# Final norm and stores of all rows moved between the last two experts, with expert 14's rows redone by indirect DMA

## The reference, cut to what matters

```python
def expert_choice_ffn(h, w_router, w_gate, w_up, w_down):
    b, n, d = h.shape
    cap = CAPACITY_FACTOR * n // N_EXPERTS          # 64 latent rows, 16 context rows for each expert
    aff = jax.nn.softmax(jnp.einsum('bnd,de->bne', h, w_router).astype(jnp.float32), axis=-1)
    gates, idx = lax.top_k(jnp.swapaxes(aff, 1, 2), cap)
    xe = jax.vmap(lambda hb, ib: hb[ib])(h, idx)
    a = jnp.einsum('becd,edf->becf', xe, w_gate)
    u = jnp.einsum('becd,edf->becf', xe, w_up)
    ye = jnp.einsum('becf,efd->becd', jax.nn.silu(a) * u, w_down) * gates[..., None].astype(h.dtype)
    return jax.vmap(lambda yb, ib: jnp.zeros((n, d), yb.dtype).at[ib.reshape(-1)].add(yb.reshape(-1, d)))(ye, idx)

# in trunk_layer:          x = x + gate2 * expert_choice_ffn(h, *moe_w)
# in reference, at the end: y_prompt = rms_norm(xp, g_final);  y_sample = rms_norm(xs, g_final)
```

## Time and profile before

| what | value |
| --- | --- |
| median of 3 runs | 1146.9 us (1146.23 to 1149.08) |
| the profiled execution's own time | 1145.81 us |
| its span | 1144.0 us |
| PE busy | 1097.6 us, 96% of the span |
| DVE, ACT, POOL busy | 46%, 32%, 12% |
| mean DMA rate | 258 GB/s over the span, about 405 GB/s while the experts run |
| last matmul of the experts starts | 1123.3 us after the span's start |
| last DMA issue on POOL starts | 1135.10 us |

### The profile page before, as it was taken

How to read it: one execution, slowest core, us unless ns; L and a number is a source line. 1 busy time by engine, 2 the same in 40 slices (tenths; PEclk the granted TensorE clock), 3 DMA queues, 4 the chain that set the end, 5 groups by cost and what they waited for, 6 DMA issues and landing times.

```text
span 1144.0 us, 28118 instructions
## 1 busy us (share of the span) xinstructions
PE 1097.6 (96%) x12524; PEld 828.2 (72%) x12524; DVE 528.1 (46%) x961; ACT 363.2 (32%) x846; POOL 132.4 (12%) x173
## 2 busy tenths in 40 slices
PE   6999999999999999999998999999999999999993
PEld 4679875666677777777877877777777777777761
DVE  4574538879958142334976033332233223333235
ACT  4333327778753223022163221222222222211103
POOL 2332300000000000002012111111110111110021
PEclk9999999999999999999999999999999999999997
DMA  9932242111031545359987999999999999999993
GB/s 359 299 107 68 77 84 63 35 31 41 1 109 38 184 147 147 106 190 300 355 303 320 402 398 406 407 405 409 414 406 405 408 404 408 405 408 405 410 321 143
DMA packets 86747, 295.32 MB, mean 258 GB/s; under 512 B 27249, under 2 KB 28530, under 8 KB 62050
## 3 DMA queue, kind: packets, MB, share of 16 engines
q1 hardware_dynamic: 79104, 269.77, 61.5%
q0 software_dynamic: 6528, 20.10, 6.1%
q10 hardware_dynamic: 994, 3.65, 0.9%
HBM read 273.25 MB, written 15.00 MB: 252 GB/s over the span
## 4 chain that ended last, share of the span: by engine, by line
PE 85%; DMA 7%; issue 2%; ACT 2%; DVE 2%; SPq 1%; POOLq 0%; POOL 0%; ACTq 0%; DVEq 0%
PE ps L1207 39%; PE ps L772 10%; PE ps L774 9%; PE ps L773 9%; PE ps L994 4%; PE ps L1013 3%; PE ps L1032 2%; PE ps L1036 2%; DMA x_dram<-y_row,rows_t 2%; DMA x_dram<-xn_p 1%; DMA raw_first<-in_w_in_dram 1%; DMA x_f<-x_dram 1%; PE ps L794 1%; DMA raw<-in_w_in_dram 1%; PE ps L978 1%
## 5 line engine op out<-in xcount | busy, mean ns | idle before, releaser
L2124 DVE SCALAR_TENSOR_TENSOR y_row<-ps,gates,gate_q 32x256 f32<-32x256 f32 (+1 forms) x184 | 88.3, 480 | 238.5 <-PE ps L1207 236.0
L1564 ACT ACTIVATE h_t<-ps 128x256 f32<-128x256 f32 x48 | 15.0, 384 | 374.7 <-PE ps L1207 374.7
L772 PE MATMUL ps<-w_hi,ht 128*128 128x512 f32 (+1 forms) x320 | 124.2, 388 | 0.6 <-DVE q_n L1728 0.6
L774 PE MATMUL ps<-w_hi,ht 128*128 128x512 f32 (+1 forms) x320 | 121.8, 381 | 0.0
L773 PE MATMUL ps<-raw_lo,ht 128*128 128x512 f32 (+1 forms) x320 | 121.7, 380 | 0.0
L1207 PE MATMUL ps<-late,xe 128*32 128x256 f32 x1824 | 103.6, 379 | 0.0
L537 DVE TENSOR_TENSOR raw_lo<-raw,w_hi 128x1024 fp32r<-128x1024 f32 x48 | 58.2, 1234 | 78.9 <-ACT w_hi L532 78.2
L1207 PEld LDWEIGHTS ps<-late,xe 128*32 128x32 f32 x1824 | 77.0, 110 | 23.3
L1207 PE MATMUL ps<-raw,xe 128*32 128x256 f32 x1392 | 88.1, 379 | 0.9 <-issue 0.8
L532 ACT ACTIVATE w_hi<-raw 128x1024 fp32r<-128x1024 f32 x48 | 48.7, 1053 | 123.6 <-DMA raw<-in_w_in_dram 68.1
L2354 POOL DMA_INDIRECT xg<-x_dram,rows x48 | 46.1, 961 | 320.7 <-PE ps L1207 293.2
(11 more groups left out here) (315 smaller groups left out, 1831.0 us busy)
## 6 DMA issues: line engine op xcount, KB each, us to landing
late<-in_w_exp_down_dram SPq DMA_DIRECT2D x25, 1024.0 KB, 20.4
late<-in_w_exp_up_dram SPq DMA_DIRECT2D x21, 1024.0 KB, 28.8
late<-in_w_exp_gate_dram SPq DMA_DIRECT2D x17, 1024.0 KB, 24.7
raw<-in_w_in_dram SPq DMA_DIRECT2D x16, 1024.0 KB, 5.5
raw<-in_w_exp_gate_dram SPq DMA_DIRECT2D x16, 1024.0 KB
raw_gate<-in_w_exp_up_dram SPq DMA_DIRECT2D x14, 1024.0 KB
raw<-in_w_exp_up_dram SPq DMA_DIRECT2D x13, 1024.0 KB
raw_gate<-in_w_exp_down_dram SPq DMA_DIRECT2D x13, 1024.0 KB
```

The lines of the kernel that those rows point to most:

```text
L772: pe.matmul(b, stat_hi(k, tt), hi[:, kk, :], start=first, stop=False)
L774: mm = pe.matmul(b, stat_lo(k, tt), hi[:, kk, :], start=False, stop=last)
L2124: return dve.scalar_tensor_tensor(y_row[n % 2][32 * v:32 * v + count, 256 * q:256 * q + 256], bank(b, o, o + 256, src), gates[src, n % EG, ...
```

## The change

The loads of all rows, their norm and their stores now stand between experts 14 and 15. ACT starts the five `x_f` loads when PE is done with up 14 and when scatter 13 has landed; until then they waited for scatter 14. Therefore `x_f` has not got expert 14's share, and the stored rows of expert 14 are wrong at first. Its 80 rows are dealt with as those of expert 15 are: POOL gathers them into a new tile, `x_m`, after scatter 14, ACT and DVE norm them, and POOL stores them over the rows that SP stored.

What comes with it: scatter 14 waits until all five `x_f` loads have landed (they must not see it half done). POOL's stores of `x_m` wait for all stores of `x_f` (`s_cout`, `s_yout`), and every store of expert 15's rows now waits for the landing of both `x_m` stores (`s_mout`), since a row may belong to both. `finish_rms` still stands behind `silu(15)` on ACT, but `finish(0)` to `finish(4)` stand ahead of `activations(15)` on DVE. The final gain `g_fin` is loaded before scatter 14. Some tiles have other places in SBUF.

```diff
-        x_f = at("x_f", 97280, [P, NT, D])
-        x_l = at("x_l", 57344, [P, D])
-        g_fin = at("g_fin", 143360, [P, D])
+        x_f = at("x_f", 105472, [P, NT, D])
+        x_m = at("x_m", 97280, [P, D])
+        x_l = at("x_l", 101376, [P, D])
+        g_fin = at("g_fin", 57344, [P, D])
...
             for n in range(NE):
+                if n == NE - 1:
+                    act.wait_ge(s_half, done("u", NE - 2))
+                    act.wait_ge(s_scat, 16 * (NE - 2))
+                    for t in FINISH_ORDER:
+                        act.dma_start(x_f[:, t, :], x1_dram[t * P:(t + 1) * P, :]).then_inc(s_x[t], 16)
                 silu(n)
...
-            act.wait_ge(s_scat, 16 * (NE - 1))
-            for t in FINISH_ORDER:
-                act.dma_start(x_f[:, t, :], x1_dram[t * P:(t + 1) * P, :]).then_inc(s_x[t], 16)
             for i in range(NT):
                 finish_rms(i)
+            act.wait_ge(s_xm, 16)
+            act.activation(sq_l[0:EROWS, :], x_m[0:EROWS, :], ACT.Square, accum_out=ss_l[0:EROWS, 6:7]).then_inc(s_msq, 1)
+            act.wait_ge(s_msq, 1)
+            act.activation(ss_l[0:EROWS, 7:8], ss_l[0:EROWS, 6:7], ACT.Sqrt, bias=eps[0:EROWS, :], scale=1.0 / D)\
+               .then_inc(s_msq, 1)
...
+            for i in range(NT):
+                finish(i)
             activations(NE - 1)
-            finish(0)
-            finish(1)
+            dve.wait_ge(s_msq, 2)
+            dve.reciprocal(ss_l[0:EROWS, 7:8], ss_l[0:EROWS, 7:8]).then_inc(s_dve, 1)
+            dve.wait_ge(s_dve, own())
+            dve.scalar_tensor_tensor(x_m[0:EROWS, :], x_m[0:EROWS, :], ss_l[0:EROWS, 7:8], g_fin[0:EROWS, :], ALU.mult, ALU.mult)\
+               .then_inc(s_mrs, 1)
             context_added()
-            finish(2)
-            finish(3)
+            latents_added(0)
             context_scaled()
-            latents_added(0)
-            finish(4)
             latents_scaled(0)
...
+            for t in range(NT):
+                pool.wait_ge(s_x[t], 32)
+            scatter(NE - 2)
             last = NE - 1
             pool.wait_ge(s_scat, 16 * last)
             pool.wait_ge(s_rows, 5)
+            pool.indirect_dma_start(x_m[0:EROWS, :], None, x1_dram[:, :],
+                                    bass.IndirectOffsetOnAxis(ap=rows_t[0:EROWS, last - 1:last], axis=0)).then_inc(s_xm, 16)
...
             pool.wait_ge(s_cout, 16)
+            pool.wait_ge(s_yout, 16 * NTL)
+            pool.wait_ge(s_mrs, 1)
+            pool.indirect_dma_start(y_sample[0], bass.IndirectOffsetOnAxis(ap=rows_t[0:CAPL, last - 1:last], axis=0),
+                                    x_m[0:CAPL, :], None).then_inc(s_mout, 16)
+            pool.indirect_dma_start(y_prompt[0], bass.IndirectOffsetOnAxis(ap=rows_c[0:CAPC, 0:1], axis=0),
+                                    x_m[CAPL:EROWS, :], None).then_inc(s_mout, 16)
+            pool.wait_ge(s_mout, 32)
             pool.wait_ge(s_lrs, 1)
...
-            pool.wait_ge(s_yout, 16 * NTL)
```

More of the change, by code:

```diff
@@ L268, in build @@
         rows_t = sb("rows_t", [P, NE], U32)
-        rows_c = sb("rows_c", [P, 1], U32)
+        rows_c = sb("rows_c", [P, 2], U32)
         ss_l = sb("ss_l", [P, 10])
@@ L385, in build @@
         bias_q = at("bias_q", 61440, [P, 256])
-        x_f = at("x_f", 97280, [P, NT, D])
-        x_l = at("x_l", 57344, [P, D])
-        sq_l = at("sq_l", 81920, [P, D])
-        g_fin = at("g_fin", 143360, [P, D])
+        x_f = at("x_f", 105472, [P, NT, D])
+        sq_f = at("sq_f", 125952, [P, D])
+        x_m = at("x_m", 97280, [P, D])
+        x_l = at("x_l", 101376, [P, D])
+        sq_l = at("sq_l", 141312, [P, D])
+        g_fin = at("g_fin", 57344, [P, D])
         x_lq = at("x_lq", 8192, [P, 2, 256])
@@ L445, in build @@
         s_lrs = sem("s_lrs"); s_lout = sem("s_lout")
+        s_xm = sem("s_xm"); s_msq = sem("s_msq"); s_mrs = sem("s_mrs"); s_mout = sem("s_mout")
         s_fss = sem("s_fss"); s_frs = sem("s_frs"); s_fy = sem("s_fy")
@@ L1583, in finish_rms @@
                     act.wait_ge(s_fss, i)
-                act.activation(squares2[:, :], x_f[:, t, :], ACT.Square, accum_out=ss[:, t:t + 1]).then_inc(s_fss, 1)
+                act.activation(sq_f[:, :], x_f[:, t, :], ACT.Square, accum_out=ss[:, t:t + 1]).then_inc(s_fss, 1)
                 act.wait_ge(s_fss, i + 1)
@@ L2086, in _ @@
             dve.tensor_copy(rows_t[0:EROWS, :], bank(4, NE, 2 * NE, slice(0, EROWS))).then_inc(s_rows, 1)
-            dve.tensor_scalar(rows_c[0:CAPC, :], bank(4, 3 * NE - 1, 3 * NE, slice(0, CAPC)), -float(LAT), None, ALU.add)\
+            dve.tensor_scalar(rows_c[0:CAPC, :], bank(4, 3 * NE - 2, 3 * NE, slice(0, CAPC)), -float(LAT), None, ALU.add)\
                .then_inc(s_rows, 1)
@@ L2372, in _ @@
             fetch(2)
-            for n in range(NE):
+            for n in range(NE - 1):
                 if n:
@@ L2378, in _ @@
             pool.dma_start(g_fin[:, :], g_final.rearrange("(a n) -> a n", a=1).to_broadcast([P, D])).then_inc(s_gfin, 16)
+            pool.wait_ge(s_half, done("u", NE - 2))
             for q in range(4):
@@ L2390, in _ @@
             pool.wait_ge(s_cout, 16)
+            pool.wait_ge(s_yout, 16 * NTL)
[5 more added lines that the diff above has]
+            pool.wait_ge(s_mout, 32)
             pool.wait_ge(s_lrs, 1)
-            pool.indirect_dma_start(y_prompt[0], bass.IndirectOffsetOnAxis(ap=rows_c[0:CAPC, :], axis=0),
+            pool.indirect_dma_start(y_prompt[0], bass.IndirectOffsetOnAxis(ap=rows_c[0:CAPC, 1:2], axis=0),
                                     x_l[CAPL:EROWS, :], None).then_inc(s_lout, 16)
-            pool.wait_ge(s_yout, 16 * NTL)
             y_quarters = y_sample[0].rearrange("t (q n) -> (t q) n", q=4)
```

## The result

The changed kernel takes 1151.15 us (median of 15 runs, 1150.15 to 1152.67), the kernel before 1147.18 us (15 runs, 1146.10 to 1149.08). The ratio is 1.0035, interval 1.0028 to 1.0043: slower by 4.0 us, where 1.4 us were predicted. The profiled execution has a span of 1149.1 us against 1144.0. Of these 5.1 us, 0.7 are there long before the change comes into play: scatter 13 starts at 1074.49 and not at 1073.76. The last store of expert 15's rows is issued at 1140.10 and not at 1135.10, 5.0 us later, so the tail itself accounts for 4.3.

A forecast was written before the change was run, and what follows sets the result against it. The tail was taken as the bound, through POOL's last store of expert 15's rows: landing at 1138.9 against 1137.5, with `x_f` stores 4.1 us earlier and 5.5 us for two stores and a wait. +1.4 on 1146.9 gave 1148.3 us, range 1143.0 to 1152.5.

The forecast's parts named there:

- Late gathers: Rival: scatter 14 behind loads landing at 1109, last gather taking 9.7 us; +5.4, 1152.3 us; chance 0.23.
- G: Landing of the gathers of expert 15's rows, taken as 1125; it would decide the end from 1128.2 on.
- signs that it is wrong: Scatter 14 out before 1100, `x_f` stores landed under 1126 or over 1132, or DVE's last scaling later than 1136.
- The loads of `x_f`: ACT issues them at 1083, not 1104.8; sharing packet against packet with weights, they take 18.8 us and land about 1105.5.
- Scatter 14: POOL's scatter of expert 14, ready at 1095.74, waits for the loads until 1105.7 and lands 9.0 later, 1114.7.
- The gathers: Four POOL gathers after scatter 14, 1.3 us apart, 1115.0 to 1119.0; `x_m` lands near 1121, the last at 1125.
- Two more stores and a wait: POOL's `x_m` stores and the wait for their landing cost 5.5 us at the end; last store lands at 1138.9.
- Y: Landing of all `x_f` stores, which POOL waits for: 1129.2 predicted against 1133.32 before.
- The stores of `x_f`: SP issues them at 1105 to 1112, behind the last weights; all landed at 1129.2, a gain of 4.1 us.
- Stores mix with the weights: Variant: SP's stores served beside the last weights, PE ends at 1133.3; +1.6, 1148.5 us; chance 0.57 including the forecast.
- The last weights and PE's end: Expert 15's last weight chunk 3.2 us later, at 1118.9, PE ends at 1126.8; about 3 us are covered.
- The finish between the experts: ACT squares about 9 us, to 1110; DVE is free at 1111.4; nothing lost, or 0.2 us.

The follow-up runs named there:

- Experiment 4: Changed kernel with four of the five `x_f` tiles loaded and stored in pairs, 8 KB per partition in a row: 1148.15 us, ratio 1.0008.
- Experiment 1: Changed kernel with DVE's four context pieces of expert 15 ahead of the norm of `x_m`: 1148.91 us, ratio 1.0018.
- experiment 8: Changed kernel without gather, norm and stores of `x_m`: 1146.23 us, ratio 1.0000.
- experiment 7: Kernel before with only the `x_m` gather, norm, stores and wait added; loads, finish and scatter 14 at their old place: 1155.02 us, ratio 1.0073.
- experiment 3: Changed kernel with the `x_f` loads reading the kernel's inputs, so scatter 14 need not wait for them: 1150.04 us, ratio 1.0022.

## Why the prediction was off, by its steps

The forecast was +1.4 us, "no visible change"; measured were +4.0, just beyond the 3.4 us from which it called a change visible. The range 1143.0 to 1152.5 holds the 1151.15, but partly by luck, since the forecast had POOL's chain as the bound and DVE's was it. Of the rival "Late gathers" one half came true: the loads were in at 1108.7 and DVE's chain was the bound. The other half did not: the last gather took about 4.6 us and not 9.7, and G stayed under the 1128.2 from which it was to decide. Of the prediction's signs that it is wrong one came: DVE's last scaling began at 1139.15, later than 1136. Step by step:

*The loads of `x_f`.* Issued at 1083.74: right. The prediction let them share packet against packet at 0.47 us per pair, and as a mean over all packets that price was right too. From 1086 to 1103 us the changed kernel's queues show

```profile
q1 hardware_dynamic: 623, 4.52, 65.8%
q10 hardware_dynamic: 580, 2.13, 32.0%
```

which is 16 x 17 / 580 = 0.47 us per packet and engine. The count was wrong. I took 40 packets per engine, 640 rows of 4 KB over 16 engines. The whole of the loads, 1083 to 1109 us, is

```profile
q10 hardware_dynamic: 720, 2.62, 25.6%
```

which is 45 per engine, as the earlier trace rows had it for the stores of the same five tiles. 2.62 MB are 640 x 4 KB, so the other 80 carry next to nothing; they are one for each of five DMAs on each of 16 engines (the Trainium skill, "DMA: Bandwidth & Descriptors", Why a DMA increments its semaphore by 16 and not by 1, has each engine count the completion for itself). Experiment 4 bears the count out: three DMAs, 48 more. The prediction left them out of the weights as well: the earlier trace rows have 687 packets, 43 per engine, where it counted 38 (in that window 77 packets are under 512 bytes). That the extra packets take turns like the others is my reading; the 0.47 us is a mean over both kinds, and counted by 4 KB rows alone (2.13 MB are 520) it is 0.52 us a row. The trace does not say whether the extra packets cost a turn or the rows more each. 1085.57 + 45 x 0.47 + 1.5 = 1108.2; landed at 1108.70. Either way 2.3 of the 3.2 us by which the landing missed 1105.5 are here, and the row with the 720 stood in the prediction's own groups.

*Scatter 14.* 9.60 us where 9.0 was taken, out at 1109.67, landed at 1119.27 and not at 1114.7.

*The gathers: the size that failed.* "`x_m` itself lands near 1121" and G at 1125. Both came out of the loads' landing and of gathers that share with the stores only. Measured: `x_m` after 7.04 us at 1126.57, where 6 us were taken; 4.5 of its 5.6 us of lateness are the late issue behind scatter 14 and 1.0 is its own. G is at 1127.9, 2.9 us late. From 1119 to 1126 the gathers passed 217 packets beside 325 of the stores of `x_f`, and the first of the four gathers landed only 1.3 us before the last. G at 1127.9 alone would have been covered: the prediction put its turning point at 1128.2, and the run without the route has G = 1127.5 and the time of before.

*The step that failed as a mechanism.* "Its 1.5 us on ACT and 1.5 us on DVE are over at 1124 and hold up the context rows, which wait for G anyway." They did not wait for G; they waited for the norm. With `x_m` landing 1.3 us before G, DVE's part of the norm (1128.10 to 1129.57) and the four pieces behind it (2.0 us) lie behind G, and the add comes 3.8 us behind it. The sum of this step: x_l's add at 1131.66 less the 0.7 of the start is 1131.0, against a predicted 1125, so 6.0 us late; DVE's chain had 3.2 us of slack against POOL's (1133.3 against 1136.5); 6.0 - 3.2 = 2.8, and 1.4 + 2.8 = 4.2 us, against 4.3 in the trace's tail and 4.0 in the medians. Experiment 1 took 2.2 us of it back by order alone. What the gather that stands in front of the others (1.28 us of POOL) costs beside the norm was not separated by a run of its own, but two traces bear on it. Counted from scatter 13, G is at 53.4 us both in the changed kernel (the estimate above) and without the route. The cost of the route lies behind G: the add comes 3.8 us behind it in the changed kernel, and 0.1 us in experiment 8.

*Two more stores and a wait: right in size, wrong as the bound.* From the first to the last store 6.9 us were predicted and 6.8 measured, in experiments 4 and 7, where Y releases the first of them. In the changed kernel `x_m` was not ready before 1129.57, POOL's chain ends before DVE's, and taking the stores away gave 0.3 us.

*The stores of `x_f`.* Y was predicted at 1129.2. The stores' queue passed its last packets before 1126.5, so they landed by about 1127, 6 us before the 1133.32 of the earlier trace rows. The gain was real and larger than forecast; nothing waited for it. Why it was larger was not tested. The rule of the Trainium skill ("DMA: Bandwidth & Descriptors", Queues, rings and completion order) that each engine takes one queue's descriptors in ring order bears here: in experiment 3 the last of the five stores was issued at 1113.56 and landed at 1130.34, 6.1 us behind the last weights on the same queue. That trace agrees, and the variant "Stores mix with the weights" fell.

*The last weights and PE's end.* PE waited for `w_in_hi` until 1119.52 (predicted 1118.9). Its end was 1130.1 and not 1126.8, for the most part for a reason of its own. The changed kernel's stretches (length, busy of PE, PEld, DVE, ACT, POOL, granted clock, DMA share, GB/s):

```profile
1115.00:1119.00 4.00, 1.07 (x16) 0.42 (x16) 0.00 (x0) 0.00 (x0) 0.00 (x0) 1.00 0.62 210
1119.00:1123.00 4.00, 3.48 (x36) 1.70 (x40) 0.00 (x0) 0.00 (x0) 2.85 (x3) 0.57 0.69 256
1123.00:1127.00 4.00, 3.54 (x67) 2.45 (x61) 0.00 (x0) 0.41 (x1) 0.95 (x1) 1.00 0.74 259
```

and the kernel before, where PE had been busy 3.44 of the 4 us from 1115, in the second of them:

```profile
1119.00:1123.00 4.00, 4.00 (x80) 2.39 (x76) 3.68 (x7) 3.67 (x8) 0.00 (x0) 1.00 0.81 324
```

Behind a wait of 3.43 us the granted clock stood at 0.57 of full, which is mostly the lower of its two levels (1.2 GHz), and the 32 matmuls of `w_in_hi` took 3.48 us where they took 1.93. That is 1.6 us; about 1 us more lies in gaps between the later groups, which I did not trace. It cost nothing, since DVE takes the second latent set only at 1136.5. The estimate "about 3 us of this are covered" was too small for the same reason that DVE was late.

*The finish between the experts.* ACT's squares ran from 1101.45 to 1110.2 (predicted: 9 us, until 1110), DVE's from 1104.5 to 1111.7 and nothing waited for them: right.

## What to carry to other kernels

When a group of transfers is moved forward beside a saturated stream, count its packets per engine in the trace and price each with one packet of the other queue; then follow not only what waits for the moved group, but what now stands behind it (here a scatter and four gathers, 14 us later than before). Before a bound is called covered by slack, put every instruction that stands in that engine's order between the last arrival and the end into the sum: here a norm, set ahead of 2.0 us of work that was ready, turned 3.2 us of slack into the bound. A step that removes one late wait gains nothing if the chain beside it ends at the same place; without the new route the changed kernel and the kernel before take the same time.

## What the runs showed of the hardware that was not expected

The DMA engines divide themselves by packets and not by bytes: 174 packets of loads beside 175 of weights with 0.65 and 1.27 MB, and 185 beside 179 with 1.12 and 1.32 MB once the loads' rows were 8 KB long. With the same 2.62 MB to move, scatter 14 went out 5.0 us earlier, and the kernel took 3.0 us less; the loads were fewer packets too (432 against 720), and these two were not separated. The prediction used the sharing as given; the row length turned out to be a way to set it.

Behind one wait of 3.43 us TensorE's granted clock stood at 0.57 for 4 us; in experiment 3, with several waits of 0.5 to 1.9 us, it stood at 0.77 and 0.50 in the two stretches from 1119 to 1127. A late weight can cost more than its lateness: 1.6 us of slower matmuls on top of 3.43 us of waiting. It need not. In experiment 7, after a wait of 2.29 us, the same 32 matmuls ran at the full clock (the row of the stretch as above):

```profile
1119.38 1.93 PE L1210 MATMUL ps<-w_in_hi,ht 128*32 128x256 f32 x32 [2.29 <-DMA w_in_hi<-in_w_exp_down_dram]
```

```profile
1119.00:1123.00 4.00, 3.62 (x68) 2.24 (x72) 2.02 (x3) 2.18 (x4) 0.00 (x0) 1.00 0.67 265
```
